# Two-layer hybrid decoder trunk on one core: VectorE's steps cut in two around the weight remainder, memory products one row earlier

## What is computed

```python
def even_layer(h, ...):
    p = rms_norm(h, norm_g) @ w_in
    qkv_a, z_a, b_a, a_a, glu_b, z_b, q_m, z_m = jnp.split(p, cuts, axis=-1)
    qkv = silu(causal_depthwise_conv(qkv_a, conv_qkv))
    q, k, v = heads(qkv)                       # 8 heads of 128
    o = gated_delta_rule(q, k, v, beta, g)     # chunked, with a triangular solve
    o_a = rms_norm(o, dn_norm_g) * silu(z_a)
    c = causal_depthwise_conv(glu, dw_w) + dw_b          # 31 taps
    o_b = silu(layer_norm(c, ln_g, ln_b)) * silu(z_b)
    o_m = memory_attend(q_m, z_m, q_norm_m, mem_k, mem_v)
    return concatenate([o_a, o_b, o_m], axis=-1) @ w_out

def memory_attend(q_m, z_m, q_norm_g, mem_k, mem_v):    # 4 heads of 256, 256 memory tokens
    s = einsum('bshd,bmhd->bhsm', rms_norm(q_m), mem_k) * (MEM_HEAD_DIM ** -0.5)
    return einsum('bhsm,bmhd->bshd', softmax(s), mem_v) * silu(z_m)
```

## Time and profile before

| | us |
|---|---|
| runs (3): median, lowest, highest | 1313.81, 1313.45, 1314.37 |
| the profiled execution | 1314.93 |
| its span, first to last instruction | 1313.2 |
| TensorE busy | 1305.3 |
| VectorE busy | 988.5 |
| ScalarE busy | 747.6 |
| GpSimd busy | 90.0 |

### The profile page before, as it was taken

One profiled execution on the slowest core, in us unless ns is written; L12 is line 12 of the kernel. 1 busy time (PEld: TensorE's weight loads), 2 busy tenths in 40 slices (PEclk: granted clock), 3 DMA queues, 4 the chain that ended last, 5 costly groups with the idle time before them and its releaser, 6 DMA issues.

```text
span 1313.2 us, 17465 instructions
## 1 busy us (share of the span) xinstructions
PE 1305.3 (99%) x6317; PEld 1097.7 (84%) x6317; DVE 988.5 (75%) x1548; ACT 747.6 (57%) x1173; POOL 90.0 (7%) x91
## 2 busy tenths in 40 slices
PE   9999999999999999999999999999999999999998
PEld 8898889988888888788888888888888888888887
DVE  5468588898988898887667477797788788667663
ACT  5556643576445645586346447748657568555341
POOL 2000200103000100100001020020110200000000
PEclk9999999999999999999999999999999999999999
DMA  8675565765965996685668665765765766978552
GB/s 298 212 210 179 156 198 159 192 209 166 268 179 179 314 299 204 206 252 175 202 204 260 208 191 152 244 194 165 235 198 166 234 193 191 278 216 227 194 193 80
DMA packets 177807, 271.79 MB, mean 207 GB/s; under 512 B 38160, under 2 KB 59577, under 8 KB 177721
## 3 DMA queue, kind: packets, MB, share of 16 engines
q1 hardware_dynamic: 175001, 265.95, 66.5%
q10 hardware_dynamic: 2720, 4.72, 1.1%
HBM read 250.57 MB, written 20.05 MB: 206 GB/s over the span
## 4 chain that ended last, share of the span: by engine, by line
PE 95%; DVE 2%; DMA 2%; ACT 1%; SPq 0%; issue 0%; POOL 0%; ACTq 0%; POOLq 0%
PE job L1983 55%; PE job L1993 27%; PE job L1980 2%; DMA raw<-in_ev_w_in_dram 2%; PE job L1990 1%; PE mixer L2205 1%; PE mixer L2193 1%; DVE wlo L1457 1%; PE mixer L2115 1%; PE mixer L2004 1%; DVE cvr L1724 1%; PE mixer L2215 1%; PE mixer L2223 1%; PE mixer L2095 1%; PE mixer L2128 1%
## 5 line engine op out<-in xcount | busy, mean ns | idle before, releaser
L1983 PE MATMUL job<-whi,xhi 128*128 128x512 f32 x1628 | 647.7, 398 | 0.0
L1983 PE MATMUL job<-whi,xlo 128*128 128x512 f32 x1628 | 634.5, 390 | 0.0
L1457 DVE TENSOR_TENSOR wlo<-raw,whi 128x1024 fp32r<-128x1024 f32 x431 | 527.2, 1242 | 81.5 <-ACT whi L1088 80.3
L1088 ACT ACTIVATE whi<-raw 128x1024 fp32r<-128x1024 f32 x431 | 444.5, 1055 | 215.6 <-PE job L1993 179.7
L1993 PE MATMUL job<-wlo,xhi 128*128 128x512 f32 x1628 | 435.5, 389 | 0.0
L1993 PEld LDWEIGHTS job<-wlo,xhi 128*128 128x128 f32 x1628 | 305.6, 188 | 64.2
L1983 PEld LDWEIGHTS job<-whi,xhi 128*128 128x128 f32 x1628 | 305.9, 188 | 61.4
L1983 PEld LDWEIGHTS job<-whi,xlo 128*128 128x128 f32 x1628 | 306.0, 188 | 61.1
L1724 DVE SCALAR_TENSOR_TENSOR cvr<-cvr,vt 128x255 f32<-128x255 f32 (+14 forms) x240 | 97.9, 465 | 0.0
L1121 ACT ACTIVATE proj<-job,rstd 128x512 f32<-128x512 f32 x74 | 46.6, 683 | 62.2 <-PE job L1993 42.9
L1490 DVE TENSOR_TENSOR hid<-hid,job 128x512 f32<-128x512 f32 x46 | 29.5, 682 | 42.6 <-PE job L1993 39.4
(11 more groups left out here) (307 smaller groups left out, 970.0 us busy)
## 6 DMA issues: line engine op xcount, KB each, us to landing
raw<-in_od_w_in_dram SPq DMA_DIRECT2D x160, 512.0 KB, 4.2
raw<-in_ev_w_in_dram SPq DMA_DIRECT2D x143, 512.0 KB, 4.5
raw<-in_ev_w_out_dram SPq DMA_DIRECT2D x48, 512.0 KB, 5.5
raw<-in_od_w_out_dram SPq DMA_DIRECT2D x48, 512.0 KB, 5.3
raw<-in_w_mem_kv_dram SPq DMA_DIRECT2D x32, 512.0 KB, 4.8
proj<-turned_blocks SPq DMA_DIRECT2D x68, 128.0 KB, 5.0
turned_blocks<-proj SPq DMA_DIRECT2D x9, 512.0 KB, 4.9
turned_blocks<-mix SPq DMA_DIRECT2D x7, 512.0 KB, 4.3
```

Source lines behind the costliest of these rows:

```text
L1088: act(whi[:, c % RING, :, :], raw[:, c % RAWS, :, :], ACT.Copy).then_inc(s_hi, 1)
L1457: vec.tensor_tensor(wlo[:, c % RING, :, :], raw[:, c % RAWS, :, :], whi[:, c % RING, :, :].bitcast(F32), ALU.subtract).then_inc(s_lo, 1)
L1983: mm(pj[j % 2][n][:, :], x[:, s, cols], h, start=first, stop=False)
```

## The change

Steps whose part on VectorE waits twice are cut in two. The second half is put behind the remainder of its row, or of a later row, by a stream number of 10:

- `dnV` keeps the first addition, and `dnW` (what waits for ScalarE's logarithm) goes behind the remainder.
- `dnM` is VectorE's multiplication of `dnG`, behind the remainder of the same row. TensorE's and ScalarE's parts of `dnG` stay.
- `rsv` is VectorE's part of the second and third `rstd`, one row later, behind the remainder.
- `mqm`, `mqr`, `mkm` and `mkr` are the halves of VectorE's part of `mqs` and `mks`, with GpSimd's power between them.
- `d6f` is the last factor of `d6`, in the next row; it isn't among the ones behind the remainder.

Beside this, `ar` counts two rows instead of three and `mao` none, so that each pair of products with the values stands one row earlier; the first pair of four now stands in the row of the fourth scores. The reloads of x start one row earlier and stand two rows apart instead of four.

```diff
+SECOND = ("dnM", "dnW", "rsv", "mqm", "mqr", "mkm", "mkr")
@@
-            placed.append((int(pos), k, len(placed), step))
+            placed.append((int(pos), 10 if step[0] in SECOND else k, len(placed), step))
@@
-        s += [(("dnB", h0 + 3), 1), (("dnV", g), 2), (("dnR", g), 2.5)]
-        s += [(("dnG", h), 1) for h in range(h0, h0 + 4)]
+        s += [(("dnB", h0 + 3), 1), (("dnV", g), 0), (("dnW", g), 2), (("dnR", g), 2.5)]
+        for h in range(h0, h0 + 4):
+            s += [(("dnG", h), 0), (("dnM", h), 1)]
@@
-        last = [(("d6", g), 1)] + [(("gate", h), .25) for h in range(h0, h0 + 4)]
+        last = [(("d6", g), 1), (("d6f", g), 0)] + [(("gate", h), .25) for h in range(h0, h0 + 4)]
@@
-    stream(3, oa + 2, [(("xload", b), 4) for b in range(4)])
+    stream(3, oa + 1, [(("xload", b), 2) for b in range(4)])
@@
-    stream(4, oa + 1, [(("mqs", i), 1) for i in range(2)])
+    for i in range(2):
+        stream(4, oa + 1 + i, [(("mqs", i), 0), (("mqm", i), 2), (("mqr", i), 0)])
@@
-        stream(4, ks, [(("mks", b), 0)])
+        stream(4, ks, [(("mks", b), 0), (("mkm", b), 1), (("mkr", b), 0)])
@@
-        return [[(("mas", n), 2), (("mat", n), 0), (("aw", n), 2), (("ar", n), 3), (("mao", 2 * n), .5), (("mao", 2 * n + 1), 0)]
+        return [[(("mas", n), 2), (("mat", n), 0), (("aw", n), 2), (("ar", n), 2), (("mao", 2 * n), 0), (("mao", 2 * n + 1), 0)]
@@
-    stream(5, max(CH0[J_MEM] - 6, q + 2), [(("rstd", 1), 0)])
+    stream(5, max(CH0[J_MEM] - 6, q + 2), [(("rstd", 1), 1), (("rsv", 1), 0)])
@@
-            def do_dnG(h):
+            def do_dnM(h):
                 ve.wait_ge(s_eq, h + 1)
                 v = aq[:, 2 * (h % 4):2 * (h % 4) + 2, :, :].rearrange("p m c n -> p (m c n)")
                 vec.tensor_tensor(v, M[0][:, :], v, ALU.mult).then_inc(s_aq, 1)
@@
+            def do_mqm(i):
+                ve.wait_ge(s_mqs, order[i])
                 vec.tensor_scalar(qss[:, i, :], qss[:, i, :], 1.0 / 256, EPS, ALU.mult, ALU.add).then_inc(s_mqm, 1)
+            def do_mqr(i):
+                ve.wait_ge(s_mqr, order[i])
                 vec.tensor_scalar(qrs[:, i, :], qss[:, i, :], 1.0 / 16, None, ALU.mult).then_inc(s_mqk, 1)
```

More of the change, by code:

```diff
@@ L136 @@
 CONV_ROOM = 0.2
+SECOND = ("dnM", "dnW", "rsv", "mqm", "mqr", "mkm", "mkr")
 CONV_SHARE = 0.31
-VECTOR_SHARE = {"evac": .5, "dnC": 1.3, "dnU": .5, "dnV": .35, "dnR": .25, "dnG": .4, "inF": 2.7, "inT": 1.0, "d4y": .55, "d5c": .15,
+VECTOR_SHARE = {"evac": .5, "dnC": 1.3, "dnU": .5, "dnV": .35, "dnR": .25, "dnM": .4, "inF": 2.7, "inT": 1.0, "d4y": .55, "d5c": .15,
                 "d5e": .1, "d6": .25, "gate": .25, "za": .45, "glu": .45, "zg": .65, "lt": .47, "nt": .5, "xt": .18, "mf": .16, "bas": .1}
@@ L325, in make_plan @@
         stream(5, CH0[J_ODIN] + 4 + (k - 12) // 2, [(("xt", F_H + k), 0)])
-    stream(5, CH0[J_ODIN] + 1, [(("rstd", 2), 0)])
+    stream(5, CH0[J_ODIN] + 1, [(("rstd", 2), 1), (("rsv", 2), 0)])
     stream(6, CH0[J_ODIN] + 4, [(("sbk", 0), 0)])
@@ L337, in make_plan @@
         stream(5, after(J_ODIN + 4 * g + 3) - 1, [(("zb", 4 * g + i), 1) for i in range(4)])
-    p = stream(6, max(p + 1, after(J_ODIN + 17)), [(("mqs", 2), 1), (("mqs", 3), 1)])
+    p = max(p + 1, after(J_ODIN + 17))
+    for i in (2, 3):
+        stream(6, p, [(("mqs", i), 0), (("mqm", i), 2), (("mqr", i), 0)])
+        p += 1
     for e in (8, 9):
@@ L1583, in do_dnV, with do_dnW @@
                 vec.tensor_scalar(hln[:, g, :, :], nrm[:, hs, :], 4 * EPS, None, ALU.add).then_inc(s_lnq, 1)
+            def do_dnW(g):
+                hs = slice(4 * g, 4 * g + 4)
                 ve.wait_ge(s_lnq, 2 * g + 2)
@@ L1690, in do_d6, with do_d6f @@
                 vec.tensor_scalar(oms[:, g, :], oms[:, g, :], 1.0 / 128, EPS, ALU.mult, ALU.add).then_inc(s_oms, 1)
+            def do_d6f(g):
+                sq = ex[:, g, 3, :]
                 ve.wait_ge(s_opw, g + 1)
@@ L1840, in do_zg, with do_mkr @@
                     ins.then_inc(s_z, 1)
-            mq_n = [0]
-            def mean_squares(i):
-                mq_n[0] += 1
-                n = mq_n[0]
-                ve.wait_ge(s_mqs, n)
+            def do_mqm(i):
+                ve.wait_ge(s_mqs, order[i])
                 vec.tensor_scalar(qss[:, i, :], qss[:, i, :], 1.0 / 256, EPS, ALU.mult, ALU.add).then_inc(s_mqm, 1)
-                ve.wait_ge(s_mqr, n)
-            def do_mqs(i):
-                mean_squares(i)
+            def do_mqr(i):
+                ve.wait_ge(s_mqr, order[i])
                 vec.tensor_scalar(qrs[:, i, :], qss[:, i, :], 1.0 / 16, None, ALU.mult).then_inc(s_mqk, 1)
-            def do_mks(i):
-                mean_squares(4 + i)
+            def do_mkr(i):
+                ve.wait_ge(s_mqr, order[4 + i])
                 for t in range(T):
@@ L1924, in do_sbo @@
                                          ).then_inc(s_sbo, 1)
-            steps = {"rest": rest, "half": do_half, "evac": do_evac, "first": do_first, "xt": do_xt, "mf": do_mf, "rstd": do_rstd,
+            steps = {"rest": rest, "half": do_half, "evac": do_evac, "first": do_first, "xt": do_xt, "mf": do_mf, "rstd": lambda i: None if i else do_rsv(i),
                      "baw": do_baw, "bat": do_bat, "bas": do_bas,
                      "za": do_za, "dnC": do_dnC,
-                     "dnU": do_dnU, "dnV": do_dnV, "dnR": do_dnR, "dnG": do_dnG, "inF": do_inF, "inT": do_inT,
-                     "d4y": do_d4y, "d5c": do_d5c, "d5e": do_d5e, "d6": do_d6, "gate": do_gate, "glu": do_glu,
-                     "conv": do_conv, "lnx": do_lnx, "lnv": do_lnv, "lnr": do_lnr, "lna": do_lna, "lno": do_lno, "zb": do_zb, "zT": do_zT, "zg": do_zg, "lt": do_lt, "nt": do_nt, "mqs": do_mqs,
-                     "mks": do_mks, "mas": do_mas, "mat": do_mat, "mao": do_mao, "sbn": do_sbn, "sbB": do_sbB, "sbz": do_sbz, "sbc": do_sbc, "sbo": do_sbo}
+                     "dnU": do_dnU, "dnV": do_dnV, "dnR": do_dnR, "dnM": do_dnM, "dnW": do_dnW, "inF": do_inF, "inT": do_inT,
+                     "d4y": do_d4y, "d5c": do_d5c, "d5e": do_d5e, "d6": do_d6, "d6f": do_d6f, "gate": do_gate, "glu": do_glu,
+                     "conv": do_conv, "lnx": do_lnx, "lnv": do_lnv, "lnr": do_lnr, "lna": do_lna, "lno": do_lno, "zb": do_zb, "zT": do_zT, "zg": do_zg, "lt": do_lt, "nt": do_nt, "mqm": do_mqm, "mqr": do_mqr, "rsv": do_rsv,
+                     "mkm": lambda i: do_mqm(4 + i), "mkr": do_mkr, "mas": do_mas, "mat": do_mat, "mao": do_mao, "sbn": do_sbn, "sbB": do_sbB, "sbz": do_sbz, "sbc": do_sbc, "sbo": do_sbo}
             for st, i in plan:
```

2 lines of the change are left out of this document (1 added, 1 removed).

## The result

| | before | after |
|---|---|---|
| median of 6 runs each, on one chip | 1314.49 us | 1319.51 us |
| lowest and highest | 1313.45, 1314.99 | 1318.41, 1321.35 |
| the profiled execution, its span | 1314.93, 1313.2 | 1319.41, 1317.7 |

The changed kernel is slower: ratio 1.0042, 95% interval 1.0031 to 1.0052, or 5.0 us. The forecast was 1318.8 us. The time is inside its range, and the sign is right. As will be shown, that it lies so near is in part luck: errors in the sum partly cancelled.

The account below looks back on a forecast made before the run. TensorE, busy 1305.3 of 1313.2 us, was taken as the bound. Terms 5.3 + 0.1 - 0.6 = +4.8 us, or 5.0 with a little for mao0, on the 1313.81 median gave 1318.8 us; range 1316.3 to 1322.5.

Parts of the forecast that it names:

- First group, 0 us: Rows of dnG0 to dnG3: the remainder fits VectorE's 2.6 us idle time before dnM, hidden under ScalarE's exponentials; 0 us.
- Stall of 3.0 us before dnG7: Second group: dnM6 ends at 326.72, so TensorE's dnG7, needing its two banks, starts at about 326.78 instead of 323.76.
- The pause before the first inversion product: Second group's inversion: TensorE waits 2.9 us instead of 0.6 us before its first product.
- dnM7 7.4 us later: Second group: dnM7 on VectorE, behind za1, lt16 and the remainder, ends at 334.37 instead of 326.96.
- inA at 3.2 instead of 4.5 us: Store of the matrices after dnM7: it meets an empty queue, so it takes 1.3 us less.
- The shift at the first inversion product, 5.3 us: Second group's inversion: 7.4 us late dnM7, less 0.8 us slack and 1.3 us from inA; includes the 3.0 us stall.
- a bound of 3.9 us for a quick inC: Shift at the first inversion product if inC's store takes 3.2 us instead of 4.65 us.
- dnM4, 0.1 us with 0.45 as the bound: Second group: dnM4 ends 1.5 us later where dnG5 had 1.04 us to spare; 0.1 us taken, 0.45 at most.
- The LayerNorm gain, -0.6 us: Before the product of the LayerNorm sums: the chain gets about 0.6 us shorter, of a 0.9 us wait.
- mao0 and xload, 0 us: Memory products and reloads of x: earlier placement costs 0 us; mao0 1 us at most, reloads hidden by the weight ring.
- rival (b): TensorE's clock falls after its two 3 us pauses: 1.9 us each, up to 3.8 together, 1320.7 to 1322.6; chance 0.12.
- The sign that the prediction set for (b): A digit under 9 in the page's clock row behind either TensorE pause would show the clock had fallen.

## Why the prediction was right, and where its steps weren't

- **First group, 0 us**: right. The kernel with only that group moved is as fast as the one with none.
- **Stall of 3.0 us before dnG7**: right, 2.93 us, and it goes with dnM6. The pause before the first inversion product was put at 2.9 us and is 2.36.
- **dnM7 7.4 us later**: right. It starts 6.7 us later, in a trace that was 0.9 us ahead.
- **inA at 3.2 instead of 4.5 us**: right. From its issue to inB's it took 3.20 us in the changed kernel, and 3.2 in all nine kernels with a late dnM6 or dnM7 that were profiled; it took 4.5 to 4.7 in all five without. In those five, the kernel before among them, a weight load was issued in the microsecond ahead of it, and in the nine none for over 5 us. That fits the queue that the prediction took as the reason, which nothing tested by itself.

```profile
333.69 0.37 SPq L866 DMA_DIRECT2D dn_matrices<-hid  x1
336.89 0.62 SPq L870 DMA_DIRECT2D mix<-dn_matrices  x1
...
346.78 0.61 SPq L878 DMA_DIRECT2D dn_block_inverses<-mix  x1
...
350.77 0.37 SPq L885 DMA_DIRECT2D mix<-dn_block_inverses  x1
```

- **The shift at the first inversion product, 5.3 us**: 5.0 measured (4.1 by the rows, plus the 0.9 that the trace was ahead). The size is right, and the last part of the reasoning is not. "Of inC and inD I change nothing" treated them as links of the path, with a bound of 3.9 us for a quick inC. inC did get quicker (3.99 instead of 4.65 us), but VectorE's rows above show no wait for it: behind the inversion the path is VectorE's own backlog, with the transfers 0.4 us behind it as a close second. It carried on the lateness of the inversion's start (5.7 us: 7.6 for dnM7, less 0.8 of slack and 1.3 of inA, and 0.2 more for inB), less 0.7 us of waits that VectorE had there before, 0.40 of it for a weight copy. The estimate by the Trainium skill ("DMA: Bandwidth & Descriptors", section "Anatomy of one DMA — SWDGE (gpsimd) path") gave 2.15 us for inC's 64 KB and would have made the shift 2.8. That section is on transfers issued by GpSimd, and these are SyncE's. Over the fourteen profiled kernels inC took 3.0 to 6.1 us, so the trace doesn't agree there; for inA's 512 KB the same rule's 3.2 us agrees where no load had just been issued. A quicker inC would not have made the shift smaller here, since inD already landed before VectorE came to it.
- **dnM4, 0.1 us with 0.45 as the bound**: 0 in the changed kernel, 0.5 without the rest of the change. The reason given, dnW1's wait, wasn't tested by itself.
- **The LayerNorm gain, -0.6 us**: mis-sized. The whole wait of 0.9 us went, and the trace gains 1.2 us. The term assumed that ScalarE's next copy would take back a third of it. The 0.7 us that the rest of the change gains at the first inversion product, seen with dnM at the head of its rows, the prediction didn't have; the late dnM covers them. The two together are 1.9 us by the trace, over the 1.5 that the prediction gave as the most.
- **mao0 and xload, 0 us**: right, ratio 0.9998 for them alone.
- **The clock**: here the forecast's mechanism failed, though its number held. "The clock falls" was rival (b), priced 1.9 us a pause, with a chance of 0.12, beside a forecast that had the clock at full. It is the rule, not the exception: 0 of 16 runs of the three kernels with both pauses kept a mean of 1.000, and each of their three traces has one stretch at the lower clock behind one of the two pauses. One stretch costs 1.5 to 1.7 us by the traces, where the rival had 1.9. Behind the other pause the clock stayed up, so the rival's 3.8 us for both was too much. The weight was wrong: the only evidence was "at full after every short wait", which, as the prediction wrote itself, "shows nothing on long ones", a pause three times as long. The Trainium skill names the mechanism ("TensorE: Matmul & The Clock Gate", section "HAM oscillation — how this bites in real kernels"): an idle TensorE is throttled to half its clock and the next products start cold. The trace agrees, by a granted clock of 0.51 and by 0.63 us for a product of 0.40. The waits in that section's example are 3 to 5 us long; here 2.9 and 2.4 us were enough.

The sum over the trace is thus 3.1 + 1.9 + 1.6 - 1.2 = 5.4 us, where the prediction had 5.3 + 0.1 - 0.6 = 4.8. The first two terms (5.0 for 5.3) were good. The clock left out (+1.6), the gain put too low (-0.6) and the shift put too high (-0.3) partly cancel; and these two traces differ by 0.9 us at the program's start besides, which isn't the change's. That the time landed on the forecast for a sum that lacked its third largest term is in part luck.

The sign that the prediction set for (b), a digit under 9 in the clock row, would have missed it: in every one of these traces the row is all nines. Windows of a few microseconds behind the pauses show it.

What would be worth keeping of the change: all but the second group's dnM. With dnM at the head of its rows in both groups the kernel takes 1312.79 us, ratio 0.9987 to the kernel before, and with the first group's behind the remainder 1312.24 against 1313.71, ratio 0.9990. Both are faster than either kernel here; the two can't be told apart.

## To carry over

Before a step is put behind "the remainder", list everything else that stands in that row and whether it waits for a third engine: the remainder cost 1.1 us, the gate behind ScalarE's tanh and the taps cost 1.8 us at the first of the two places, and a bank, a transfer and a block inversion hung on the step. Follow the engine's order behind a late step to where it has no more waits; from there its backlog can pass the lateness on even where a transfer is faster, and moving a step later in the same order moves its end as well. And where an edit makes TensorE stand still for longer than the trace before shows anywhere, add the lower clock behind each such pause to the sum, and look for it in narrow windows.

## What the runs showed of the hardware

The granted clock fell to its lower level (0.51 in a stretch) behind single pauses of 2.9 and 3.1 us, and of 2.4 us where one of 2.9 stood 31 us ahead, in an engine otherwise 99% busy, and was up again some 3.4 us later; 1.5 to 1.7 us were lost each time. It doesn't always fall: behind the same 2.9 us before dnG7 the changed kernel's trace keeps the clock and the trace with dnM6 alone loses it. With shorter pauses (1.8 and 1.0 us) at least two and at most five of nine runs lost it, and none of 44 runs without a pause did. The clock was also low in the last microsecond or so of six traces, behind TensorE's last product, where it costs nothing and still lowers the mean.

Small transfers vary from kernel to kernel by more than the effects looked for: inC's store of 64 KB took 3.0 to 6.1 us, while inA's 512 KB, with no load issued just ahead, took 3.2 us nine times out of nine.
